# Seven more seven-product pairs in a hybrid trunk's input projection, the head groups in another order beside them, and some first accumulator writes on ScalarE

## The chip, the core and the metric

The kernel runs on one core of one Trainium2 chip. The metric is device time in microseconds (us) for one launch. TensorE (PE) multiplies, VectorE (DVE) and ScalarE (ACT) work on PE's results and on operands, GpSimd (POOL) prepares weights, SyncE (SP) issues most of the DMA transfers, ACT issues the rest from its own instruction stream. Every engine works through its instructions in order, and the orders are fixed when the kernel is built; a semaphore wait at one instruction holds everything behind it on that engine.

## What is computed

One layer of a trunk on x (1024 x 2048): a norm, one wide projection, three groups of heads, an output projection with residual, a final norm.

```python
h = rmsnorm(x, norm_gain)
proj = jnp.einsum('bsd,de->bse', h, w_in)              # 59 column tiles of 128
aq, af, ai, ag, bq, bk, bv, bg, cq, ck, cv, cg = split_columns(proj)
ya = hgrn2_group(aq, af, ai, lb, hgrn_gain) * jax.nn.silu(ag)      # A: 6 heads, recurrence
yb = band_attention_group(bq, bk, bv, rel_bias) * jax.nn.silu(bg)  # B: 5 heads, softmax
yc = retention_group(cq, ck, cv, cos, sin) * jax.nn.silu(cg)       # C: 5 heads, retention
y = jnp.concatenate([ya, yb, yc], axis=-1)
x = x + jnp.einsum('bse,ed->bsd', y, w_out)
return rmsnorm(x, final_gain)
```

An A head needs four column tiles (f, q, v, gate), a B head four (q, k, v, gate), a C head three (q and k together, v, gate).

## The kernel before

**Products.** Every large product is computed in three passes, high by high, low by high, high by low, with the operands split into `_hi` and `_lo`. A matmul instruction multiplies a 128x128 weight block by 512 columns. The tokens are two halves of 512 columns, the contraction is 16 row blocks of 128. A plain tile (128 output columns, all tokens) therefore takes 16 x 2 x 3 = 96 matmuls. A *pair* of tiles can be computed by a seven-product scheme (7 products of half the contraction, on half the tokens): 7 x 8 x 3 = 168 matmuls in place of 192. It needs sums and differences of weight blocks and of h blocks as operands, and adds the products up in accumulators in SBUF (`acc_in`).

**Stage 1** (`in_product`, L800): 15 pairs, so 105 steps of one product each, two *granules* of weights (four 128x128 blocks) per step. Product j is done for all 15 pairs in turn, since all share the operand set `in_hi[j%2]`, `in_lo[j%2]`, whose h combinations are built in SBUF for one j and overwritten for j+2. For weights with two terms (products 0 to 4 of the seven) POOL adds the terms (L753), ACT makes w_hi (L1203), DVE makes w_lo (L1697); for one-term weights POOL makes w_lo (L760). DVE accumulates (`in_accumulate`, L1747 to L1761). SP stores finished accumulators to `z_scratch`.

**Rows of h.** The plain tiles need the 16 h rows (`mv_hi`, `mv_lo`). In the last steps of stage 1 SP loads each row of x into an accumulator that its store has left (`load_x`, L572), ACT makes the high part (`h_high`, L1243), DVE the low part (`h_low`, L1766).

**Plain tiles beside the heads** (`project`, L821): the other 29 tiles, each cut into 8 *slots* of 12 matmuls. After a slot PE does whatever head stage a table has put there (`put`, L1046): A head u from slot 20u-4 on (`A_FROM`, `A_EACH`), B heads each 12 slots from slot 121, C heads at 183, 192, 201, 210 and the last at 223 to 231. An A head has one diagonal product (`a_diag`), seven levels (`a_level`), transposes, state, output and two half sums of squares (`a_ss`); between the levels DVE makes the next operand pair and drains the last result (`lv_next`, `lv_drain`). A C head has key transposes (`c_ktr`), scores, value transposes, state, output, and two half sums of squares (`c_ss`, L851 and L852). Its key is rotated first: ACT makes `partner`, DVE `rotate` (L2095 to L2099), and these stand behind the previous head's norm and gating (L1930, L1936) and an eviction (L1648). Head inputs come back from `z_scratch` by DMAs that ACT issues (`load_z`, L1262); tiles of stage 1 are scaled by rstd before they are stored, plain ones after they land (`landed`, L1655).

**Then** the output projection, in seven-product pairs as well (L1092), and the final norm.

## Time and profile before

| | us |
|---|---|
| median of 3 runs | 1776.33 (1775.26 to 1777.37) |
| the profiled execution | 1775.74 |
| its span in the trace | 1773.9 |
| PE busy | 1743.0 (98%) |
| DVE, POOL, ACT busy | 1107.9, 763.1, 626.4 |
| stage 1: PE from 8.5 to about | 603 |
| plain tiles beside the heads | about 603 to 1440 |

The profile is a page for one execution: busy time of each engine, the span in forty slices with the clock that PE was granted, the DMA queues, the chain of waits that ended last, and groups of instructions by code line. The trace behind it answers for single instructions: start, duration, and, in brackets, how long the engine was idle before and what released it. A duration printed for a matmul is longer than the distance to the next one, since they are pipelined; the distance between starts is what counts.

### The profile page before, as it was taken

The page shows a single profiled execution, that of the slowest core. Times are in us where ns is not written, and L with a number is a line of the kernel's source. Part 1 is how long each engine was busy: PE and PEld are TensorE (multiplying, and loading weights), DVE is VectorE, ACT ScalarE, POOL GpSimd, SP SyncE. Part 2 cuts the span into 40 slices and gives each one's busy share as a digit, 9 for nine tenths or more (in the row PEclk, how much of TensorE's full clock was granted, in tenths as well). Part 3 has the DMA queues.
Part 4 walks back from the last instruction along what each step waited for, and adds up shares of the span by engine and source line. Part 5 has one row for each costly group of instructions (what it writes and reads, how often), then busy time and mean ns, then how long its engine had stood idle before and what let it go on. Part 6 is the DMA issues. An engine that isn't in the chain of part 4 may idle for free.

```text
span 1773.9 us, 27559 instructions
## 1 busy us (share of the span) xinstructions
PE 1743.0 (98%) x10704; PEld 1444.8 (81%) x10704; DVE 1107.9 (62%) x1641; ACT 626.4 (35%) x923; POOL 763.1 (43%) x545
## 2 busy tenths in 40 slices
PE   7999999999999999999999999999999999999996
PEld 6888888888888788887887888888888877888885
DVE  6857665554668766565555356555655448778886
ACT  4423344332435132231331233333544233333442
POOL 4544444444455544334344433333334430355452
PEclk9999999999999999999999999999999999999998
DMA  7767777685988523323323332233433369778876
GB/s 252 231 226 255 241 236 256 226 261 179 301 268 271 168 71 126 101 74 109 113 72 102 127 109 85 96 96 112 133 117 102 93 207 344 256 247 264 282 248 230
DMA packets 160710, 323.08 MB, mean 182 GB/s; under 512 B 18362, under 2 KB 19135, under 8 KB 160580
## 3 DMA queue, kind: packets, MB, share of 16 engines
q1 hardware_dynamic: 146314, 276.26, 47.7%
q10 hardware_dynamic: 14266, 45.05, 7.2%
q8 instruction: 86, 1.41, 0.3%
q14 instruction: 44, 0.36, 0.1%
HBM read 275.08 MB, written 46.15 MB: 181 GB/s over the span
## 4 chain that ended last, share of the span: by engine, by line
PE 95%; DVE 2%; ACT 1%; DMA 1%; issue 0%; POOL 0%; SPq 0%; DVEq 0%; ACTq 0%; POOLq 0%
PE prj L821 36%; PE prj L800 32%; PE prj L1092 15%; PE mix L960 2%; PE mix L943 2%; PE mix L840 1%; PE mix L885 1%; PE mix L953 1%; PE mix L913 1%; PE mix L916 1%; PE mix L902 1%; PE mix L1013 1%; PE mix L991 1%; PE mix L1016 0%; PE mix L1002 0%; DVE arena L2245 0%
## 5 line engine op out<-in xcount | busy, mean ns | idle before, releaser
L767 POOL TENSOR_SCALAR w_hi<-w_sum 128x512 fp32r<-128x512 f32 x119 | 189.5, 1592 | 502.5 <-DMA w_sum<-in_w 490.6
L800 PE MATMUL prj<-in_hi,w_hi 128*128 128x512 f32 x840 | 329.7, 392 | 9.5 <-DVE w_lo L1697 8.5
L800 PE MATMUL prj<-in_lo,w_hi 128*128 128x512 f32 x840 | 328.4, 391 | 0.0
L800 PE MATMUL prj<-in_hi,w_lo 128*128 128x512 f32 x840 | 328.3, 391 | 0.0
L821 PE MATMUL prj<-mv_hi,w_hi 128*128 128x512 f32 x928 | 300.7, 405 | 1.8 <-DVE mv_lo L1766 1.8
L753 POOL TENSOR_TENSOR w_sum<-in_raw,in_raw 128x512 f32<-128x512 f32 x150 | 202.4, 1350 | 211.0 <-PE prj L800 201.1
L821 PE MATMUL prj<-mv_lo,w_hi 128*128 128x512 f32 x928 | 287.4, 391 | 0.0
L821 PE MATMUL prj<-mv_hi,w_lo 128*128 128x512 f32 x928 | 286.2, 390 | 0.0
L821 PEld LDWEIGHTS prj<-mv_lo,w_hi 128*128 128x128 f32 x928 | 174.2, 188 | 38.1
L821 PEld LDWEIGHTS prj<-mv_hi,w_lo 128*128 128x128 f32 x928 | 174.2, 188 | 38.0
L800 PEld LDWEIGHTS prj<-in_hi,w_hi 128*128 128x128 f32 x840 | 158.5, 189 | 44.0 <-issue 8.9
L821 PEld LDWEIGHTS prj<-mv_hi,w_hi 128*128 128x128 f32 x928 | 163.2, 188 | 29.4 <-DVE mv_lo L1766 2.2
L800 PEld LDWEIGHTS prj<-in_lo,w_hi 128*128 128x128 f32 x840 | 158.7, 189 | 33.5 <-issue 0.5
L800 PEld LDWEIGHTS prj<-in_hi,w_lo 128*128 128x128 f32 x840 | 158.7, 189 | 33.1
L1697 DVE TENSOR_TENSOR w_lo<-w_sum,w_hi 128x512 fp32r<-128x512 f32 x150 | 115.8, 775 | 111.5 <-ACT w_hi L1203 107.9
L776 POOL TENSOR_TENSOR raws<-raws 128x512 f32<-128x512 f32 x80 | 111.8, 1399 | 164.5 <-DMA raws<-in_wo 164.5
L769 POOL TENSOR_TENSOR w_lo<-w_sum,w_hi 128x512 fp32r<-128x512 f32 x124 | 171.2, 1381 | 22.8 <-ACT w_hi L1526 12.9
L1092 PE MATMUL prj<-mv_hi,w_hi 128*128 128x512 f32 x448 | 175.1, 391 | 3.8 <-POOL w_lo L769 1.2
L1092 PE MATMUL prj<-mv_lo,w_hi 128*128 128x512 f32 x448 | 174.4, 389 | 0.0
L1092 PE MATMUL prj<-mv_hi,w_lo 128*128 128x512 f32 x448 | 174.3, 389 | 0.0
L1203 ACT ACTIVATE w_hi<-w_sum 128x512 fp32r<-128x512 f32 x150 | 93.8, 628 | 175.3 <-POOL w_sum L753 175.2
L760 POOL TENSOR_TENSOR w_lo<-in_raw,w_hi 128x512 fp32r<-128x512 f32 x60 | 81.4, 1357 | 82.5 <-ACT w_hi L1203 82.4
(175 smaller groups left out, 2371.8 us busy)
## 6 DMA issues: line engine op xcount, KB each, us to landing
in_raw<-in_wi SPq DMA_DIRECT2D x360, 256.0 KB, 3.2
raws<-in_wo SPq DMA_DIRECT2D x184, 256.0 KB, 3.9
...
```

The costliest lines, as they stand in the source:

```text
L753: nc.gpsimd.tensor_tensor(w_sum[wslot(n)][:], in_raw_buf(a), in_raw_buf(b), ALU.add if sign > 0 else ALU.subtract).then_inc(in_wsum, 1)
L760: nc.gpsimd.tensor_tensor(w_lo[wslot(n)][:], in_raw_buf(m), w_hi[wslot(n)][:].bitcast(F32), ALU.subtract).then_inc(w_split, 1)
L767: nc.gpsimd.tensor_scalar(w_hi[q][:], w_sum[q][:], 1.0, None, ALU.mult).then_inc(w_hi_done, 1)
L769: nc.gpsimd.tensor_tensor(w_lo[q][:], w_sum[q][:], w_hi[q][:].bitcast(F32), ALU.subtract).then_inc(w_split, 1)
L776: nc.gpsimd.tensor_tensor(raw_buf(a), raw_buf(a), raw_buf(b), ALU.add if sign > 0 else ALU.subtract).then_inc(wsum_done, 1)
L800: last = nc.tensor.matmul(out, wt[wslot(n)][:, i % GRAN, :], mv[j % 2][:, i, :], start=(i == 0 and wt is w_hi and mv is in_hi), stop=(i == ...
L821: last = nc.tensor.matmul(prj[pair][:, half(side)], wt[wslot(q)][:, kk, :], mv[:, k, half(side)], start=(k == 0 and wt is w_hi and mv is m ...
L943: last = nc.tensor.matmul(mix[0][:, out_at + lo:out_at + hi], arena_r[:, wt, p * P:p * P + P], arena_r[:, mv, keys], start=(wt == BQH and ...
L960: last = nc.tensor.matmul(mixb(1)[:, 5, :], blocks(V)[:, p + 1 - nk + j, :], blocks(BT[p % 2])[:, j, :], start=(j == 0), stop=(j == nk - 1))
L1092: last = nc.tensor.matmul(bank(s), wt[wslot(W0 + n)][:, i % GRAN, :], slot(mv, j, i), start=(i == 0 and wt is w_hi and mv is mv_hi), stop= ...
L1203: nc.scalar.activation(w_hi[wslot(n)][:], src, ACT.Copy).then_inc(in_w_hi, 1)
L1697: tt(w_lo[wslot(n)][:], src, w_hi[wslot(n)][:].bitcast(F32), ALU.subtract).then_inc(w_split, 1)
```

## The change

Seven further pairs (`MID_PAIRS`) are computed by the seven-product scheme, after stage 1, and only 15 plain tiles are left. The operand sets for it are those of stage 1: they are stored to a DRAM scratch (`comb_scratch`, 7 x 8 x 2 blocks of 256 KB) while stage 1 uses them, and loaded back into `mv_hi`/`mv_lo` for the middle part. The middle part has 49 steps, 98 slots; with 15 x 8 = 120 plain slots the slot table has 218 entries in place of 232. Head stages now stand in the middle part's slots too, in a new order: B heads at slots 2 to 61, C heads 0 to 2 at 64, 72, 80, then the A heads at 89, 108, 125, 142, 159, 176, C head 3 at 201, and the last C head at 209 to 217. The columns of w_in are reordered to suit, and the counts of semaphores are rewritten. In the middle part POOL makes both the sum and w_lo; ACT makes w_hi and, for products 0 and 1, also writes the accumulators first (`in_first`); DVE does the other accumulations. The x rows and h rows are made at slots 88 to 103 (`H_DUE`), in the order of quarters 1, 2, 0, 3.

```diff
-A_FROM, A_EACH, B_FROM, B_EACH = -4, 20, 121, 12
-A_LATE = 2
-LEVEL_AT = [8, 9, 11, 12, 13, 15, 16]
-C_AT = [183, 192, 201, 210]
+MID_PAIRS = 7
+STD0 = IN_TILES + 2 * MID_PAIRS
+SLOTS = MID_SLOTS + 2 * NG * STD
+A_AT = [89, 108, 125, 142, 159, 176]
+LEVEL_AT = [8, 9, 10, 11, 12, 14, 15]
+LEVEL_AT_SLOW = [8, 9, 11, 12, 14, 15, 17]
+B_FROM, B_EACH = 2, 12
+C_AT = [64, 72, 80, 201]
+FIRST_ORDER = [1, 2, 0, 3]
+        H_DUE = [88, 89, 90, 91, 91, 93, 95, 97, 100, 100, 101, 101, 101, 102, 103, 103]
...
+            def store_set(j, i):
+                sp.wait_ge(in_comb_lo, HK * j + (i + 1 if j > 0 else HK))
+                for n, mv in enumerate((in_hi, in_lo)):
+                    sp.dma_start(comb_dram[j, i, n], mv[j % 2][:, i, :].bitcast(F32)).then_inc(comb_out[j % 2], 16)
...
+            load_x(HK)
+            store_mid_two(ALL_STEPS - 4)
+            load_x(HK + 1)
+            load_std_w(ALL_GRANULES)
+            store_mid_two(ALL_STEPS - 3)
+            load_x(HK + 2)
...
+            for n in range(IN_ONE, ALL_GRANULES):
+                if IN_GRANULES <= n + 1 < ALL_GRANULES and in_two(n + 1):
+                    in_weight_sum(n + 1)
+                src = w_sum[wslot(n)][:] if in_two(n) else in_raw_buf(in_raw_of[n][0])
                 pool.wait_ge(in_w_hi, n + 1)
...
-                if g < IN_TILES + 2:
-                    pe.wait_ge(in_acc_done, IN_STEPS - 1 + g - IN_TILES)
+                if g < STD0 + 2:
+                    pe.wait_ge(in_acc_done, ALL_STEPS - 2 + 2 * (g - STD0))
...
-            for slot_at, part in ((223, c_ktr), (224, c_scores), (225, c_vtr), (227, c_state), (229, c_out)):
+            for slot_at, part in ((-9, c_ktr), (-8, c_scores), (-7, c_vtr), (-5, c_state), (-3, c_out)):
+                put(SLOTS + slot_at, part(last_c))
+            for st in range(IN_STEPS, ALL_STEPS):
+                pe.wait_ge(in_acc_done, st - 3)
+                for q in range(2):
+                    mid_product(2 * st + q, range(GRAN * q, GRAN * q + GRAN))
+                    stages[2 * (st - IN_STEPS) + q]()
...
+                until(b)
+                a_z_first(u)
+                until(b + 1)
+                a_z_second(u)
+                if u == 0:
+                    load_z(a_tile(u) + 1, T1, z1_in)
+                    load_z(a_tile(u) + 2, VT, z2_in)
+                sigmoid_exp(m, Q)
+                until(b + 2)
```

On ACT, `until(slot)` puts in front of a head's next step the middle part's own work that is due by then: first writes, w_hi up to slot + 3, and h_high rows.

ACT before, where stage 1 ends and A head 0 begins (`z_clamped` to `silu_log` are the waits of that head's exponentials and logarithms, `in_raw_*` are weights of stage 1; the loads of this head's tiles stand 13 rows further up):

```order
L1243 ACTIVATE mv_hi<-acc_in,gain_sb 128x1024 [waits z_odd1]
L1137 ACTIVATE arena<-arena 128x1024 [waits z_clamped]
L1140 ACTIVATE arena<-arena 128x1024 [waits y_stored,z_exp]
L1203 ACTIVATE w_hi<-in_raw_67 128x512 [waits w_used,raw_in2]
L1203 ACTIVATE w_hi<-in_raw_68 128x512 [waits w_used,raw_in3]
L1140 ACTIVATE arena<-arena,lb_now 128x1024 [waits z_under,lb_copied]
L1137 ACTIVATE arena<-arena 128x1024 [waits z_log]
L1203 ACTIVATE w_hi<-in_raw_69 128x512 [waits w_used,raw_in4]
L1203 ACTIVATE w_hi<-in_raw_70 128x512 [waits w_used,raw_in5]
L1243 ACTIVATE mv_hi<-acc_in,gain_sb 128x1024 [waits z_odd2]
L1137 ACTIVATE arena<-arena 128x1024 [waits silu_clamped]
L1140 ACTIVATE arena<-arena 128x1024 [waits silu_exp]
```

ACT after, at the same head's beginning, which is now the end of the middle part (slots 88 to 91; `in_raw_66`, `67`, `68` are the weights of granules 303, 304, 305, that is slots 93, 94, 95):

```order
L1297 ACTIVATE arena<-arena 128x1024 [waits z_clamped]
L1300 ACTIVATE arena<-arena 128x1024 [waits z_exp]
L1363 ACTIVATE w_hi<-in_raw_66 128x512 [waits w_used,raw_in1]
L1402 ACTIVATE mv_hi<-acc_in,gain_sb 128x1024 [waits z_even2]
L1300 ACTIVATE arena<-arena,lb_now 128x1024 [waits z_under,lb_copied]
L1297 ACTIVATE arena<-arena 128x1024 [waits z_log]
L1424 DMA arena<-z_scratch 128x1024 [waits z_mid0] x2
L1297 ACTIVATE arena<-arena 128x1024 [waits silu_clamped]
L1363 ACTIVATE w_hi<-in_raw_67 128x512 [waits w_used,raw_in2]
L1402 ACTIVATE mv_hi<-acc_in,gain_sb 128x1024 [waits z_even3]
L1402 ACTIVATE mv_hi<-acc_in,gain_sb 128x1024 [waits z_mid0]
L1300 ACTIVATE arena<-arena 128x1024 [waits silu_exp]
```

The load of the head's q tile moved to right in front of the instruction that needs it, and the next w_hi (`in_raw_67`) stands behind that instruction; two h rows (`z_even3`, `z_mid0`) stand in front of the w_hi after that, which comes four instructions below the last row shown.

SP before, in the last steps of stage 1:

```order
L549 DMA in_raw_69<-in_wi 128x512 [waits w_split]
L549 DMA in_raw_70<-in_wi 128x512 [waits w_split]
L577 DMA z_scratch<-acc_in 128x512 [waits in_scaled] x2
L572 DMA acc_in<-in_xT 128x1024 [waits z_odd3]
L577 DMA z_scratch<-acc_in 128x512 [waits in_scaled] x4
L572 DMA acc_in<-in_xT 128x1024 [waits z_odd4]
```

SP after, in the last steps of the middle part (`in_acc_done` counts the steps accumulated; the four stores shown are those of steps 149, 150, 151 and, last, 152, in this order):

```order
L677 DMA z_scratch<-acc_in 128x512 [waits in_acc_done] x2
L667 DMA acc_in<-in_xT 128x1024 [waits z_even3,w_used]
L667 DMA acc_in<-in_xT 128x1024 [waits z_mid0]
L677 DMA z_scratch<-acc_in 128x512 [waits in_acc_done] x2
L667 DMA acc_in<-in_xT 128x1024 [waits z_mid1]
L709 DMA w_sum_54<-in_w 128x512 [waits w_used]
L677 DMA z_scratch<-acc_in 128x512 [waits in_acc_done] x2
L667 DMA acc_in<-in_xT 128x1024 [waits z_mid2]
L709 DMA w_sum_55<-in_w 128x512 [waits w_used]
L677 DMA z_scratch<-acc_in 128x512 [waits in_acc_done] x2
```

Both times the loads of x rows stand between stores; after, they stand behind stores of steps that are still being computed, with the first plain weights between them.

PE after, between the last half sum of squares of C head 3 (L1006, L1007) and the key transposes of the last C head (L995). Before, these transposes (L840, with the same waits) stood 36 such plain rows, six slots, behind L851 and L852; now six:

```order
L1006 MATMUL mix<-part_hi,ones 128x512 [waits parts_split]
L1007 MATMUL mix<-part_lo,ones 128x512
L976 MATMUL prj<-mv_hi,w_hi 128x512 x2
L976 MATMUL prj<-mv_lo,w_hi 128x512 x2
L976 MATMUL prj<-mv_hi,w_lo 128x512 x2
L976 MATMUL prj<-mv_hi,w_hi 128x512 x2
L976 MATMUL prj<-mv_lo,w_hi 128x512 x2
L976 MATMUL prj<-mv_hi,w_lo 128x512 x2
L995 MATMUL mix<-ident,arena 128x128 [waits mix1_drained,c_rot,const_in]
```

Five slots went out from between the two; ACT's and DVE's work between them (norm, gating, eviction, partner, rotation) is unchanged.

## Rows read from the trace of the kernel before

**Rows 1.** The page: PE's busy line; the chain that ended last.

```profile
PE 1743.0 (98%) x10704; PEld 1444.8 (81%) x10704; DVE 1107.9 (62%) x1641; ACT 626.4 (35%) x923; POOL 763.1 (43%) x545
...
PE 95%; DVE 2%; ACT 1%; DMA 1%; issue 0%; POOL 0%; SPq 0%; DVEq 0%; ACTq 0%; POOLq 0%
```

**Rows 2.** Waits of PE: line, releaser, us in total, times, longest.

```profile
PE prj L821 <- DVE mv_lo L1766: 1.8, 1, 1.8
```

**Rows 3.** Timeline, PE: start, us, line, operation, how many; plain tiles, then output projection.

```profile
807.17 0.76 PE L862 MATMUL mix<-arena 128*32 128x32 f32 x64
...
810.79 0.76 PE L885 MATMUL mix<-arena 128*32 128x32 f32 x64
...
1600.88 0.39 PE L1092 MATMUL prj<-mv_hi,w_lo 128*128 128x512 f32 x1
...
1602.01 0.39 PE L1092 MATMUL prj<-mv_lo,w_hi 128*128 128x512 f32 x1
```

**Rows 4.** Timeline, ACT, end of stage 1: h_high, an exponential, w_hi.

```profile
550.04 1.14 ACT L1243 ACTIVATE mv_hi<-acc_in,gain_sb 128x1024 fp32r<-128x1024 f32 x1
551.08 1.04 ACT L1137 ACTIVATE arena<-arena 128x1024 f32<-128x1024 f32 x1
...
553.12 0.62 ACT L1203 ACTIVATE w_hi<-in_raw 128x512 fp32r<-128x512 f32 x1
```

**Rows 5.** Timeline, DVE, end of stage 1: h_low, two accumulations.

```profile
562.91 1.28 DVE L1766 SCALAR_TENSOR_TENSOR mv_lo<-acc_in,gain_sb,mv_hi 128x1024 fp32r<-128x1024 f32 x1
...
566.64 1.28 DVE L1750 TENSOR_TENSOR acc_in<-acc_in,prj 128x512 f32<-128x512 f32 x2
```

**Rows 6.** Source L572 (x rows, 512 KB), from issue to landing.

```profile
DMA to landing us min/median/max: 3.4/5.3/8.3
```

**Rows 7.** Source L1262 (head tiles, 512 KB), from issue to landing.

```profile
DMA to landing us min/median/max: 3.1/3.9/7.9
```

**Rows 8.** Groups by line and form, DVE: count, busy us, mean ns: drains of levels.

```profile
L1857 DVE COPY_PREDICATED arena<-level,mix 128x1024 f32<-128x1024 int8 x30 | 39.6, 1319 | 0.0
```

**Rows 9.** Timeline, all engines, from C head 3's sum to the last ktr.

```profile
1397.81 0.39 PE L851 MATMUL mix<-part_hi,ones 128*128 128x512 f32 x1
...
1400.70 1.23 DVE L1930 SCALAR_TENSOR_TENSOR arena<-mix,arena 128x1024 f32<-128x1024 f32 x1 [4.06 <-ACT arena L1137]
...
1403.11 1.22 DVE L1648 TENSOR_TENSOR arena<-prj,rstd 128x1024 f32<-128x1024 f32 x1
...
1408.70 1.23 DVE L2095 TENSOR_TENSOR arena<-arena 128x1024 f32<-128x1024 f32 x1 [4.18 <-ACT arena L1478]
...
1409.84 2.32 DVE L2096 TENSOR_TENSOR arena<-arena 128x1024 f32<-128x1024 f32 x1
...
1412.19 1.22 DVE L2099 TENSOR_TENSOR arena<-arena 128x1024 f32<-128x1024 f32 x1
...
1414.59 1.04 PE L840 MATMUL mix<-ident,arena 128*128 128x128 f32 x8
```

**Rows 10.** Timeline, PE at its start: every 0.43, from 17.73 faster.

```profile
16.88 0.63 PE L800 MATMUL prj<-in_hi,w_lo 128*128 128x512 f32 x1
...
17.73 0.53 PE L800 MATMUL prj<-in_lo,w_hi 128*128 128x512 f32 x1
```

**Rows 11.** Windows: us, busy PE, PEld, DVE, ACT, POOL; clock, DMA share, GB/s.

```profile
100.00:200.00 100.00, 100.00 (x443) 82.81 (x442) 60.87 (x90) 32.22 (x53) 49.23 (x38) 1.00 0.72 234
...
1500.00:1505.00 5.00, 5.00 (x24) 4.13 (x23) 3.72 (x7) 1.75 (x3) 0.00 (x0) 1.00 1.06 388
1012.00:1251.00 239.00, 238.60 (x1311) 200.61 (x1309) 134.59 (x245) 80.95 (x153) 84.81 (x58) 1.00 0.31 101
...
1765.00:1770.00 5.00, 0.00 (x0) 0.00 (x0) 2.78 (x5) 0.00 (x0) 2.23 (x2) 0.50 1.02 381
```

**Rows 12.** The page, groups of POOL: weight sum and w_lo.

```profile
L753 POOL TENSOR_TENSOR w_sum<-in_raw,in_raw 128x512 f32<-128x512 f32 x150 | 202.4, 1350 | 211.0 <-PE prj L800 201.1
...
L769 POOL TENSOR_TENSOR w_lo<-w_sum,w_hi 128x512 fp32r<-128x512 f32 x124 | 171.2, 1381 | 22.8 <-ACT w_hi L1526 12.9
```

More of the change, by code:

```diff
@@ L206, in arr @@
             return arena[:, n, :]
-        ones_f32 = stage[:, 0:P]
+        ones_f32 = rstd[:, 0:P]
         def blocks(n):
@@ L653, in _ @@
+            store_mid_two(ALL_STEPS - 1)
+            for k in range(HK + 4, KB):
+                load_x(k)
+            for n in range(ALL_GRANULES + NG, W0):
                 load_std_w(n)
-                g, q = divmod(n - IN_GRANULES, NG)
-                t = IN_TILES + g - 2
-                if IN_TILES <= t < DIRECT and q == (0 if t == DIRECT - 1 else 1):
+                g, q = divmod(n - ALL_GRANULES, NG)
+                t = STD0 + g - 2
+                if STD0 <= t < DIRECT and q == (0 if t == DIRECT - 1 else 1):
@@ L1041, in _ @@
                     ones_product(0)
-            stages = [nothing] * (2 * NG * STD)
+            stages = [nothing] * SLOTS
             def put(slot, *parts):
@@ new lines, in a_unit @@
+                until(b + 9)
+                if u > 0:
+                    store_y(u - 1, a_pos(u - 1))
+                until(b + 10)
+                until(b + 11)
+                sigmoid_exp(m + 1)
+                sigmoid_ln(m + 1)
+                until(b + 12)
+                sigmoid_inv(m + 1)
+                for slot in range(b + 13, b + kdtr_at - 1):
+                    until(slot)
+                if u < A_HEADS - 1:
+                    act.wait_ge(silu_done, m + 2)
+                    load_z(a_tile(u + 1) + 1, T1, z1_in)
@@ L1487, in c_unit @@
             def c_unit(i):
[L1488 to L1491 removed]
+                b, m, late, end = C_AT[i], c_silu(i), i == C_HEADS - 2, i == EARLY - 1
+                until(b)
+                if i == 0:
+                    store_y(B0 + B_HEADS - 1, B_HEADS - 1)
+                elif late:
+                    store_y(A_HEADS - 1, a_pos(A_HEADS - 1))
+                else:
+                    store_y(C0 + i - 1, c_pos(i - 1))
@@ L1513, in c_unit @@
-                norm_second(A_HEADS + i + 1)
-                norm_ln(0, M0_C + C_M0 * i + 3, 16 * (C0 + i) + 16)
-                norm_exp(0, M0_C + C_M0 * i + 3)
-                evict_until(b + 6)
+                    if end:
+                        load_z(a_tile(0), B, z0_in)
+                    else:
+                        act.wait_ge(filled[1], c_m1(i) + 2)
+                        act.wait_ge(c_qd, i + 1)
+                        load_z(c_tile(i + 1), CQK, z0_in)
+                        until(b + 2)
+                        partner(i + 1)
@@ new lines, in c_unit @@
+                until(b + 2)
+                act.wait_ge(drained[0], c_m0(i) + 2)
+                if not end:
+                    act.dma_start(dec, dec_d[i + 1]).then_inc(cdec_in, 16)
+                until(b + 3)
+                if late:
+                    sigmoid(m)
+                elif not end:
+                    load_z(c_tile(i + 1) + 1, VT, z2_in)
+                until(b + 4)
+                norm_first(1, c_m1(i) + 3, m + 1, c_norm(i))
+                until(b + 5)
+                if i < EARLY - 1:
+                    scaled_k(i + 1)
+                    act.wait_ge(silu_done, m + 1)
+                    load_z(c_tile(i + 1) + 2, T1, z1_in)
```

833 lines of the change are left out of this document (479 added, 354 removed).

## The prediction

> **What bounds the kernel now.** First the page. PE is busy 98% of the span, and the chain that ended last is PE for 95% of it [rows 1]. So removed matmuls count in full, and so does every new microsecond in which PE waits. Then the waits of PE: between 20 us and the output projection it waits once, 1.8 us, for a low h row at the point where stage 1 hands over to the plain tiles [rows 2]. So that handover and the end of the head stages have no slack to speak of before, and these are the two places to read closely. Last the timeline, for the distance between matmuls: from 1600.88 to 1602.01 are five, 0.226 us each; from the diagonal's stage at 807.17 to the next stage at 810.79 lie one slot of 12 matmuls (2.72) and the 64 small matmuls of a stage (0.90) [rows 3]. The span is 1773.9 and the execution 1775.74, 1.8 more; the median of the runs is 1776.3. I sum against 1775.7.
>
> **What goes away.** Seven pairs at 168 in place of 192 matmuls save 168 matmuls, 14 slots: 168 x 0.2267 = **-38.1**. Head stages are the same in number and form. The old 1.8 us wait [rows 2] belongs to a handover that no longer exists: **-1.8**.
>
> **The new handover, slots 88 to 106.** It now holds four things that all go through ACT and DVE in a fixed order: norm of C head 2, last steps of the middle part, all 16 h rows, and A head 0's first tiles. I walk through it with the order of the instructions in the section on the change and durations from before: a wide exponential or logarithm on ACT 1.04, w_hi 0.62, h_high 1.14, all about 0.1 less from start to start [rows 4]; h_low 1.28, a step's two accumulations 1.28 [rows 5]; a POOL w_lo 1.38 [rows 12]; x rows land 5.3 after issue (3.4 to 8.3) [rows 6], head tiles 3.9 (3.1 to 7.9) [rows 7]. Time zero is PE's end of slot 88; PE's own plan is slot 94 at 13.6, slot 98 at 24.5, level 6 of A head 0 at 54.9 (18 slots, plus the stages between).
> - C head 2's norm leaves DVE at 2.2, an accumulation and the clamps of A's f tile at 5.8. ACT does exponential and logarithm, one w_hi and one h_high, then the second pair: done at 13.2. Only now is the q tile's load issued (before it stood 13 rows ahead). It lands at 17.2; DVE scales and clamps it, 19.0.
> - ACT has been held at the sigmoid of this tile until then, and the w_hi of slot 94 stands behind it: 20.7, w_lo 22.0. PE wanted it at 13.6: 8.4 late.
> - DVE accumulates step 149 only behind the head's log f, at 22.9. SP's next x rows stand behind the store of that step: issued at 23.8, landed 29.1. ACT makes two h_high (31.3), three sigmoid parts (34.5), and then the w_hi of slot 95: w_lo at 36.4. PE has reached slot 95 at 24.7, so 11.7 more.
> - Slots 95 to 97 run to 44.5. The first plain tile waits for the accumulation of step 151, which stands behind silu, step 150 and an h row: 48.8 where the plan was 24.5, **24 late in all**. The row x10 is loaded behind the store of step 151: lands at 55, h_low at 57.3, needed three slots into the tile: 27 late.
> - From there DVE has to do up to level 6: nine h_low (11.5), two steps (2.6), some fourteen half-width operand products of 0.64 (9) [rows 5], five masked drains of 1.32 (6.6) [rows 8], the gate and v tiles. That is 33, against PE's remaining 22 or so: up to **37 late** by level 6.
>
> Part of it will overlap better than I walk it: with landings at their minimum the first plain tile comes some 6 earlier, and if no x row is late, what is left is DVE's load alone, at least 15. With landings at the maximum it is over 40. I take **+34**, near the median row, bounds 15 and 42.
>
> **The last C head.** Before, C head 3's sum of squares is on PE at 1397.81; ACT's norm frees DVE at 1400.70, the eviction runs from 1403.11, ACT's partner frees the rotation at 1408.70, and it ends at 1412.19 + 1.22 = 1413.4; the transposes start at 1414.59 [rows 9]. That is 16.8 from sum to transposes, over six slots (16.3 plus a few tenths), and nothing is lost. After there is one slot between them, 2.72 and the second sum's two matmuls, 3.2. The chain is no shorter, and it starts from the same PE instruction. PE stands still for the slack-free chain less this: 15.6 - 3.2 = **+12.4**; 11.3 if the 2.32 at 1409.84 is 1.2 next time [rows 9]. Nothing else on PE can fill it, as PE goes in order. If A5's last slots have left ACT late it is a few more.
>
> **The clock after a wait.** In the first ten microseconds of work after the idle start matmuls came every 0.43, up to 17.73 [rows 10]: 21 of them from 8.48, each 0.2 dearer, 4.2 in all. Near the end, with PE idle, the granted clock of a stretch was 0.50 [rows 11], which is 1.2 in place of 2.4 GHz. Waits of 8 to 12 us may bring that on once or twice. Nothing (the 1.8 us wait did not show it) to 8; I take one time, **+4**.
>
> **What else moves.** (a) Stage 1 stores its combinations: 112 blocks of 256 KB, 29.4 MB, and the middle part reads them back. Stage 1 moves 234 GB/s at a share of 0.72 now [rows 11]; in 8 of every 15 steps another 512 KB in some 5.4 us a step is 97 GB/s, so near 330, below the 388 seen at share 1.06. Covered, but nearly without slack at bursts: 0 to 15, I take 0. (b) B heads beside the middle part: DVE is busy 134.6 of 239 there, ACT 81, POOL 85 [rows 11]. DVE gets 2 to 4 accumulations a step instead of nothing, ACT a w_hi and some first writes, POOL 1.35 + 1.38 per slot of about 4.0 [rows 12]. All below full; 0 to 3, I take 1. (c) C heads 0 to 2 at 8 in place of 9 slots: their chain from sum to the next key is not overlapped better than before: 0 to 5, I take 2. (d) First writes on ACT in place of DVE and A heads at 17 slots in place of 20: the A heads' DVE work no longer has slack at every level; 0 to 3, taken 0. (e) Reordered columns and the new counts move no work. Together **+3**.
>
> A rule to weigh here: one of the DVE rows above took 1.23 and the next of the same form 2.32, beside a POOL instruction [rows 9]. The Trainium skill (SBUF — State Buffer, "SBUF: two separate sides") says that a DVE instruction with two SBUF inputs and a GpSimd instruction exclude each other for the whole length of the first. The two rows agree with that, as far as two rows can.
>
> **Sum.** 1775.7 - 38.1 - 1.8 + 34 + 12.4 + 4 + 3 = 1789.2; the walk of the handover leaves more room down than up, so I forecast **1787**.
>
> **Rivals.**
> - *The handover costs half* (ends on the other side). If loads land near their minimum, 3.4 and 3.1 [rows 6, 7], and DVE fills its waits, A head 0 is late by 15 to 22 only, as DVE's load alone asks. 1775.7 - 39.9 + 18 + 11.3 + 1 = **1766**. It decides itself at a handover wait below 24: above, the kernel is not faster. For it: PE hides 6 or 7 us wherever a slot boundary absorbs a wait twice counted. Against: two x-row loads stand one behind the other, each behind an accumulation. Chance 0.24.
> - *Between the two*: a handover of 24 to 30 cancels the saving, **1776**. Chance 0.10.
> - *The full saving*: both waits do not appear, because some instruction is earlier than I read it: 1775.7 - 38.1 = **1738**. The order against it is plain at the last C head. Chance 0.04.
> - *The operand sets collide with the weights.* If the stores of stage 1 push weight loads over the limit in 8 of 15 steps for seven products, or a set for the middle part (4 MB) is late, PE waits some 0.3 to 0.5 per step, 20 to 40 us: **1815**. For it: 388 GB/s is all that was seen [rows 11], at peak. Against: three raw blocks stand ahead per granule. Chance 0.10.
> - *DVE and POOL in each other's way.* With POOL busy in 2.73 of 4.0 us of a slot, five wide DVE instructions of a C head at +1.09 each [rows 9] make 5.5 for each of three C heads, and about as much for B's operand lows: +15 on top of the forecast, **1800**. It decides if DVE reaches 90% there. By the skill's rule named above it is this case. Chance 0.10.
>
> **Chances.** The forecast's own case (both waits near what I walked, 1775 to 1800) has 0.42. A measurement of this kernel tells 0.2%, 3.5 us, from no change. Faster: 0.24 + 0.04 = 0.28. Same: 0.10, the case between. Slower: 0.42 + 0.10 + 0.10 = 0.62. The range takes in the half-price handover and the DVE case and part of the operand-set case: 1760 to 1806; outside it lie the full saving and most of the collision, some 0.13, and a little for the ends.
>
> **What would show it.** (1) Matmul instructions fall by 168. (2) The waits of PE show a row for w_lo from POOL of 8 and more us near slot 94, one more at slot 95, and one for in-step accumulations or h_low before the first plain tile; their sum with A head 0's levels is 34. (3) One wait of 11 to 13 us for the rotation at c_ktr (L995), after C head 3. (4) A clock below 1.00 in a window right behind one of them. (5) Stage 1 ends at the same time as before, within 2 us. It is wrong if (2) is under 24 in sum, since the rest of the sum then gives a faster kernel; if stage 1 is longer, the transfers did it; if B's stretch has waits on DVE, the DVE case.

## The result

| | before | after |
|---|---|---|
| median of 4 runs, us | 1776.7 (1775.3 to 1777.4) | 1803.5 (1803.1 to 1804.0) |
| the profiled execution, its span | 1775.7, 1773.9 | 1803.3, 1801.5 |

The ratio after to before is 1.0152, 95% interval 1.0135 to 1.0170: 26.8 us slower. The forecast was 1787, slower by 11, with a range of 1760 to 1806. The sign and the range hold; the forecast size is less than half of what was measured.

First the page of the changed kernel (its busy line and its chain, against [rows 1]), then the waits of PE: line, releaser, us in total, times, longest.

```profile
PE 1723.3 (96%) x10536; PEld 1422.7 (79%) x10536; DVE 1172.9 (65%) x1721; ACT 680.5 (38%) x1037; POOL 846.1 (47%) x601
...
PE 52%; DVE 6%; issue 2%; ACT 2%; DMA 2%; SPq 0%; ACTq 0%; POOL 0%; DVEq 0%
```

```profile
PE mix L995 <- DVE arena L2324: 11.3, 1, 11.3
PE prj L939 <- DVE w_lo L1916: 8.9, 1, 8.9
PE mix L1040 <- DVE arena L2052: 8.8, 4, 7.7
PE prj L954 <- DVE acc_in L1971: 7.9, 2, 4.6
PE prj L976 <- DVE mv_lo L1987: 7.4, 4, 4.5
PE prj L954 <- POOL w_lo L899: 7.3, 1, 7.3
PE mix L995 <- DVE arena L2172: 1.9, 2, 0.9
PE mix L1098 <- ACT arena L1332: 1.6, 3, 0.7
```

PE has 168 matmuls fewer (10536 for 10704) and is busy 20 us less, not 38. Of the rows shown, the only one that was there before too is the start (L939, 8.9). All the others stand where before there was one wait of 1.8 [rows 2].

Where the time went can be read to a few tenths from the starts of the matmuls in PE's timeline: every twelfth large matmul starts a slot, so each slot has a length. Stage 1 ends at 587.5 (before 587.3, and not at the 603 of the table ahead of the prediction), and from the first matmul of the output projection to the end of the span it takes 328.6 (before 328.5). All of it lies between. That stretch was 858.1 long; less the 38.1 and the 1.8 it should be 818.2, and it is 885.5: **67.3 us lost**. The loss of each stretch, against the same stages' slots of before (an A head's stages cost 14.5 beyond its slots, a B head takes 50.75, a C head's nine slots 34.0), is:

| stretch | slots | over PE's own work | the prediction said |
|---|---|---|---|
| B heads | 2 to 61 | 3.9 | 1 |
| C head 0 comes in | 62 to 64 | 5.2 | nothing of its own |
| C heads 0 to 2, rest | 65 to 88 | 3.0 | 2 |
| handover to A head 0 | 89 to 107 | 38.7 | 34, and 4 for the clock |
| A heads 1 to 5 | 108 to 192 | 2.6 | 0 |
| last C head | 208 to 217 | 13.9 | 12.4 |

The two places that the prediction named, the handover and the last C head, hold 52.6 of the 67.3. PE's timeline at these places, with the idle time before a start and its releaser in brackets:

```profile
859.67 0.47 PE L954 MATMUL prj<-mv_hi,w_hi 128*128 128x512 f32 x1 [3.34 <-DVE acc_in L1971]
...
979.24 0.77 PE L954 MATMUL prj<-mv_hi,w_hi 128*128 128x512 f32 x1 [4.57 <-DVE acc_in L1971]
991.75 0.80 PE L954 MATMUL prj<-mv_hi,w_hi 128*128 128x512 f32 x1 [7.33 <-POOL w_lo L899]
...
1015.58 1.08 PE L1040 MATMUL mix<-arena 128*32 128x32 f32 x64 [7.67 <-DVE arena L2052]
...
1439.68 1.94 PE L995 MATMUL mix<-ident,arena 128*128 128x128 f32 x8 [11.26 <-DVE arena L2324]
```

Slot 88 ends at 960.9, so 979.24 is slot 94, 991.75 slot 95. ACT's timeline shows what holds the w_hi of these slots: a sigmoid's exponential (L1297) that waits for DVE's clamp, one w_hi, then two h rows that wait 7.3 for their landing, a logarithm and two exponentials (the forget gate's is one of them), and only then the next w_hi (three in one row). At slot 94 two things came last together: POOL's w_lo behind that w_hi ended at 979.14, DVE's accumulation, behind the head's log f, at 979.20.

```profile
975.52 1.06 ACT L1297 ACTIVATE arena<-arena 128x1024 f32<-128x1024 f32 x1 [2.23 <-DVE arena L1877]
976.48 0.61 ACT L1363 ACTIVATE w_hi<-in_raw 128x512 fp32r<-128x512 f32 x1
984.41 2.43 ACT L1402 ACTIVATE mv_hi<-acc_in,gain_sb 128x1024 fp32r<-128x1024 f32 x2 [7.32 <-DMA acc_in<-in_xT]
...
989.74 1.65 ACT L1363 ACTIVATE w_hi<-in_raw 128x512 fp32r<-128x512 f32 x3
```

And the clock, in windows of 5 us (busy time of PE, PEld, DVE, ACT, POOL, then granted clock, DMA share, GB/s), at the handover and at the last C head:

```profile
970.00:975.00 5.00, 4.67 (x21) 3.54 (x19) 1.43 (x2) 3.14 (x3) 0.88 (x1) 1.00 0.70 248
975.00:980.00 5.00, 0.76 (x2) 0.70 (x3) 4.90 (x6) 1.57 (x2) 1.97 (x1) 0.71 0.00 0
980.00:985.00 5.00, 4.42 (x12) 3.10 (x10) 1.59 (x2) 0.58 (x1) 0.00 (x0) 0.61 0.96 311
...
990.00:995.00 5.00, 3.25 (x8) 2.58 (x9) 5.00 (x5) 1.39 (x3) 4.57 (x3) 0.50 0.04 15
```

```profile
1440.00:1445.00 5.00, 5.00 (x17) 4.24 (x16) 2.77 (x4) 0.67 (x1) 0.00 (x0) 0.53 0.77 203
```

In 980 to 985 PE did 12 matmuls in 4.4 us, at full clock it does 12 in 2.7. Of the 38.7 that the handover lost, 27.3 are waits and the rest, some 11, are nearly all matmuls at the lower of the two clock levels (0.43 apart in place of 0.23).

### The profile page after: what moved, and what is told of

Same layout as the page of the kernel before. It is cut to its first block, busy times and chain, and to the rows that moved or that the text cites. A ratio compares the mean times of both kernels' runs of the same rounds, so it can differ in the third digit from the quotient of the medians.

```text
span 1801.5 us, 28210 instructions
## 1 busy us (share of the span) xinstructions
PE 1723.3 (96%) x10536; PEld 1422.7 (79%) x10536; DVE 1172.9 (65%) x1721; ACT 680.5 (38%) x1037; POOL 846.1 (47%) x601
## 4 chain that ended last, share of the span: by engine, by line
PE 52%; DVE 6%; issue 2%; ACT 2%; DMA 2%; SPq 0%; ACTq 0%; POOL 0%; DVEq 0%
PE prj L976 17%; PE prj L1252 15%; PE prj L954 9%; PE mix L1115 2%; PE mix L1098 1%; PE mix L995 1%; DMA acc_in<-in_xT 1%; PE mix L1040 1%; PE mix L1108 1%; PE mix L1068 1%; PE mix L1071 1%; PE mix L1057 1%; PE mix L1168 1%; DVE arena_r L2191 1%; PE mix L1146 0%
## 5 line engine op out<-in xcount | busy, mean ns | idle before, releaser
L888 POOL TENSOR_TENSOR w_sum<-in_raw,in_raw 128x512 f32<-128x512 f32 x220 | 307.3, 1397 | 294.7 <-PE prj L939 148.6
L939 PE MATMUL prj<-in_hi,w_hi 128*128 128x512 f32 x840 | 329.6, 392 | 9.9 <-DVE w_lo L1916 8.9
L939 PE MATMUL prj<-in_lo,w_hi 128*128 128x512 f32 x840 | 328.3, 391 | 0.0
L939 PE MATMUL prj<-in_hi,w_lo 128*128 128x512 f32 x840 | 328.3, 391 | 0.0
L906 POOL TENSOR_SCALAR w_hi<-w_sum 128x512 fp32r<-128x512 f32 x63 | 105.3, 1671 | 275.6 <-DMA w_sum<-in_w 246.1
L899 POOL TENSOR_TENSOR w_lo<-in_raw,w_hi 128x512 fp32r<-128x512 f32 x88 | 121.2, 1382 | 163.3 <-ACT w_hi L1363 163.3
L1363 ACT ACTIVATE w_hi<-w_sum 128x512 fp32r<-128x512 f32 x220 | 135.6, 626 | 164.6 <-POOL w_sum L888 160.4
L939 PEld LDWEIGHTS prj<-in_hi,w_hi 128*128 128x128 f32 x840 | 158.6, 189 | 44.3 <-issue 9.4
L939 PEld LDWEIGHTS prj<-in_lo,w_hi 128*128 128x128 f32 x840 | 158.7, 189 | 33.2 <-issue 0.5
L939 PEld LDWEIGHTS prj<-in_hi,w_lo 128*128 128x128 f32 x840 | 158.6, 189 | 33.2
L1252 PE MATMUL prj<-mv_hi,w_hi 128*128 128x512 f32 x448 | 175.1, 391 | 3.9 <-POOL w_lo L908 1.3
L954 PE MATMUL prj<-mv_hi,w_hi 128*128 128x512 f32 x392 | 162.3, 414 | 15.2 <-DVE acc_in L1971 7.9
L1252 PE MATMUL prj<-mv_hi,w_lo 128*128 128x512 f32 x448 | 174.3, 389 | 0.0
L1252 PE MATMUL prj<-mv_lo,w_hi 128*128 128x512 f32 x448 | 174.3, 389 | 0.0
L1916 DVE TENSOR_TENSOR w_lo<-w_sum,w_hi 128x512 fp32r<-128x512 f32 x150 | 111.9, 758 | 89.2 <-ACT w_hi L1363 86.2
L976 PE MATMUL prj<-mv_hi,w_hi 128*128 128x512 f32 x480 | 159.1, 413 | 7.7 <-DVE mv_lo L1987 7.4
L954 PE MATMUL prj<-mv_hi,w_lo 128*128 128x512 f32 x392 | 155.7, 397 | 0.0
L954 PE MATMUL prj<-mv_lo,w_hi 128*128 128x512 f32 x392 | 155.3, 396 | 0.0
L976 PE MATMUL prj<-mv_lo,w_hi 128*128 128x512 f32 x480 | 151.3, 397 | 0.0
L976 PE MATMUL prj<-mv_hi,w_lo 128*128 128x512 f32 x480 | 150.0, 394 | 0.0
L1971 DVE TENSOR_TENSOR acc_in<-acc_in,prj 128x512 f32<-128x512 f32 x176 | 114.1, 680 | 53.8 <-PE prj L939 53.7
```

The costliest lines, as they stand in the source:

```text
L888: nc.gpsimd.tensor_tensor(w_sum[wslot(n)][:], in_raw_buf(a), in_raw_buf(b), ALU.add if sign > 0 else ALU.subtract).then_inc(in_wsum, 1)
L899: nc.gpsimd.tensor_tensor(w_lo[wslot(n)][:], src, w_hi[wslot(n)][:].bitcast(F32), ALU.subtract).then_inc(w_split, 1)
L906: nc.gpsimd.tensor_scalar(w_hi[q][:], w_sum[q][:], 1.0, None, ALU.mult).then_inc(w_hi_done, 1)
L939: last = nc.tensor.matmul(out, wt[wslot(n)][:, i % GRAN, :], mv[j % 2][:, i, :], start=(i == 0 and wt is w_hi and mv is in_hi), stop=(i == ...
L954: last = nc.tensor.matmul(out, wt[wslot(n)][:, i % GRAN, :], slot(mv, j, i), start=(i == 0 and wt is w_hi and mv is mv_hi), stop=(i == HK ...
L976: last = nc.tensor.matmul(prj[pair][:, half(side)], wt[wslot(q)][:, kk, :], mv[:, k, half(side)], start=(at == 0 and wt is w_hi and mv is ...
```

## Experiments

Two theories on the handover. *Chain*: the instructions are lined up badly on ACT, and with another order the time comes back. *Load*: DVE has that much to do before level 6 of head A0, and the order matters little. All kernels below are the changed kernel with the edit shown; the gains are against its 1803.5. The kernel before, measured anew beside each group, had medians from 1774.8 to 1777.7, so a gain read across groups is good to 1 or 2 us; by the ratios to the kernel before, x1_last gains 10, x3_act 5 and x4_hand 15.

### The last C head: rotation ahead of the norm

```diff
                 until(b + 3)
                 if late:
+                    partner(i + 1)
                     sigmoid(m)
...
                     c_part_low(i, 0)
                     c_part_low(i, 1)
+                    rotate(i + 1)
...
-                    partner(i + 1)
                     scaled_k(i + 1)
```

The eviction of its first tile moves up too, behind C head 3's states.

> The changed kernel with one thing different: the last C head's q and k tile is evicted, its partner made and the rotation done before C head 3's norm and gating, not behind them. Theory (the order put the rotation behind the norm, with one slot of cover): the wait of 11.3 at the key transposes shrinks to the 0.9 that the other C heads show there for the drained bank, and with it goes the slow clock behind it; 13.9 lost in the last ten slots becomes about 1. Time 1803.5 - 12.5 = 1791. Rival (VectorE or ScalarE is short of time there anyway, so the wait only moves to C head 3's sums or to the states): less than 5 comes back, 1799 or more.

Measured: 1791.3. The last ten slots take 38.6 in place of 50.6, which is 1.9 over PE's own work; slot 207, in front of them, takes 1.1 more. The transposes wait for the bank, as those of C heads 1 and 2 do, and the matmuls behind it keep their distance:

```profile
1429.96 1.06 PE L995 MATMUL mix<-ident,arena 128*128 128x128 f32 x8 [1.73 <-DVE arena L2172]
```

So 11 of the 13.9 at this place were the rotation behind the norm, with the slow matmuls that followed the wait, and not scarce time on ACT or DVE.

### C head 0: due work between the steps of its set-up

```diff
+            until(62)
             partner(0)
+            until(63)
             act.wait_ge(filled[1], c_m1(0))
             zero_halves()
+            until(64)
             scaled_k(0)
...
+            until(62)
             dve.wait_ge(ctab_in, 32)
             rotate(0)
```

> The changed kernel with the middle part's own due work (w_hi on ScalarE, accumulations on VectorE) put in between the steps with which C head 0 is set up, where none was. Theory A: the 3.34 wait at slot 64, which the profile gives to an accumulation, and the 1.7 of slow clock behind it come from this, 1803.5 - 5 = 1798.5. Theory B (head set-up itself is late): the wait moves to C head 0's key transposes, 1803 to 1802.

Measured: 1802.9, which can't be told from 1803.5. The wait at slot 64 is gone, and PE waits at C head 0's key transposes, one slot on:

```profile
861.88 1.94 PE L995 MATMUL mix<-ident,arena 128*128 128x128 f32 x16 [3.00 <-issue]
```

Slots 62 to 64 take 13.2 for 15.2, the slots behind them 0.8 more. In the changed kernel the accumulation that the wait is named after ended at 859.64 and POOL's w_lo, behind a w_hi that stood behind the set-up, at 859.57: both due works were late. With them in front, the set-up is late. ACT's partner begins 3.4 later, and DVE's three rotation instructions take 1.23, 2.32 and 2.17 where each had taken 1.22. The likely reason, not tested by itself, is that partner, zeroing, rotation and decay of a head's keys start only when the last B visit is done, two slots before the transposes are due. Before there were two slots as well, but no w_hi and no accumulations in them.

### ACT's order alone

Three w_hi stand ahead of the sigmoid, and two h rows one slot later.

```diff
-        H_DUE = [88, 89, 90, 91, 91, 93, 95, 97, 100, 100, 101, 101, 101, 102, 103, 103]
+        H_DUE = [88, 89, 90, 92, 92, 93, 95, 97, 100, 100, 101, 101, 101, 102, 103, 103]
...
+                    for _ in range(3):
+                        in_w_high(due["hi"])
+                        due["hi"] += 1
                 sigmoid_exp(m, Q)
                 until(b + 2)
```

> The changed kernel with ScalarE's order alone altered at the handover to the A heads: the w_hi of slots 94 to 96 stand before the sigmoid that waits for a landing, and two h rows stand one slot later. Theory chain (the 38.7 us of that handover are waits lined up on ScalarE): the waits of 4.6 and 7.3 at slots 94 and 95 go and, with the slow clock behind them, 12 to 17 come back, 1787 to 1791. Theory accumulations (VectorE's accumulations and the x rows behind them set the time at which the first plain tile can start): the wait moves to slot 98, 0 to 5 come back, 1798 to 1803.

Measured: 1797.5, 6.0 back, between the two. The 12 us of waits at slots 94 and 95 are gone, and new ones stand at slot 96 (2.67, in front of the diagonal's stage) and at slots 97 and 98:

```profile
993.89 0.79 PE L954 MATMUL prj<-mv_hi,w_hi 128*128 128x512 f32 x1 [4.89 <-POOL w_lo L899]
1000.92 0.73 PE L976 MATMUL prj<-mv_hi,w_hi 128*128 128x512 f32 x2 [1.54 <-DVE acc_in L1974]
1011.86 1.08 PE L1040 MATMUL mix<-arena 128*32 128x32 f32 x64 [7.93 <-DVE arena L2055]
```

The w_hi of slots 94 and 95 was what PE met first, not what held it. The level stage in slot 98 still waits 7.9.

### ACT's order, early accumulations, early q tile

```diff
                 until(b)
+                if u == 0:
+                    load_z(a_tile(u) + 1, T1, z1_in)
+                    load_z(a_tile(u) + 2, VT, z2_in)
                 a_z_first(u)
...
+                if u == 0:
+                    steps_to(A_AT[0] + 1)
                 silu_landed(a_tile(u) + 1, a_silu(u), Q)
...
                 a_logf(u)
+                if u == 0:
+                    steps_to(b + 5)
                 until(b + 2)
```

`steps_to(slot)` does on DVE the accumulations that are due, without h rows; a third one (b + 7) follows the q tile's silu.

> As the run before it, and two more things: VectorE accumulates steps 149 to 152 as soon as it gets there, in front of head 0's next steps, so that stores and x rows go out earlier, and the q tile of A head 0 is loaded before its exponentials and not behind. Theory chain: all of the handover that is not VectorE's own load goes; VectorE was busy 70.8 of the 95 us from slot 88 to level 6 where PE needs 61, so about 10 of the 38.7 stay, 1803.5 - 28 = 1775. Theory load (VectorE and the transfers need the time anyway): at most 12 come back, 1791 or more.

Measured: 1787.5, 16.0 back, again between. The stretch from slot 89 to 106 takes 79.9 for 94.5. Its window in the changed kernel, and then in this one:

```profile
961.00:1055.00 94.00, 66.75 (x639) 51.07 (x639) 68.55 (x79) 33.19 (x35) 33.49 (x21) 0.82 0.54 184
```

```profile
960.00:1040.00 80.00, 62.71 (x650) 48.76 (x649) 71.47 (x80) 32.92 (x34) 34.67 (x22) 0.89 0.62 215
```

DVE was busy for 68.6 of 94 and is busy for 71.5 of 80. So part of the wait was order, and the rest looks like load. The next two ask that directly.

### More work for DVE, fewer landings

```diff
                 dve.wait_ge(h_hi, s + 1)
+                if s >= 4:
+                    nc.vector.tensor_reduce(extra[:, s, :], x_row(k), AX_X, ALU.max)
```

> The reordered handover of x4_hand (1787.5), and VectorE does one useless maximum over the x row (128x1024, some 1.2 us) in front of each of the last twelve low h rows: 14 us more of work for VectorE in that stretch and nothing else. Load theory (what is left of the handover, 24 us beyond PE's own work, is VectorE's work): nearly all of it shows, 1787.5 + 12 = 1799. Chain theory (what is left are waits for landings of x rows, with VectorE idle in them): it fits into the waits, 1788 to 1792.

Measured: 1794.6, 7.1 more than x4_hand, in the middle of the two expectations; the stretch to slot 107 takes 90.6 for 84.4. The added work was as large as meant (12 instructions, mean near 1.21, 14.5 in all):

```profile
L1993 DVE TENSOR_REDUCE extra<-acc_in x12: 1198/1209/1219, 988.8 to 1038.6; 128x1 f32<-128x1024 f32 x12
```

All twelve lie in the stretch, yet DVE's busy time in it rose from 71.5 to 78.9 only, by 7.4. Everything else that it does there became shorter by 7 in sum. The low h rows in that stretch, in x4_hand and then here (count, busy us, mean ns):

```profile
L1991 DVE SCALAR_TENSOR_TENSOR mv_lo<-acc_in,gain_sb,mv_hi 128x1024 fp32r<-128x1024 f32 x16 | 24.7, 1579 | 0.8 <-ACT mv_hi L1402 0.8
```

```profile
L1994 DVE SCALAR_TENSOR_TENSOR mv_lo<-acc_in,gain_sb,mv_hi 128x1024 fp32r<-128x1024 f32 x16 | 21.4, 1345 | 0.0
```

One such row took 1.28 alone [rows 5]. So the time rose by what DVE's busy time rose by (7.1 and 7.4), which is what a bound on DVE would do. That part of its busy time is the lengthening of instructions beside GpSimd's is a third theory, *contention*, for x11_whi_act below.

The counterpart takes landings away:

```diff
-                sp.dma_start(x_row(k), xT[k]).then_inc(x_row_sem(k), 16)
+                if not HK <= k < HK + GRAN:
+                    sp.dma_start(x_row(k), xT[k]).then_inc(x_row_sem(k), 16)
```

> The reordered handover of x4_hand, and x rows 8 to 11 are not loaded: ScalarE and VectorE make h rows 8 to 11 from whatever lies in those accumulators, once it has been stored. This leaves out those four transfers and their landing time of 5 us each, and nothing of the work. Chain theory: 5 to 12 come back, 1776 to 1782. Load theory: 0 to 3, 1785 to 1787.5.

Measured: 1788.7, no less than the 1787.5 with the transfers. This kernel leaves out the loading of four x rows, so it multiplies with what lay there. Four landings of 5 us each are worth nothing once the order is right. Chain falls as far as these four rows go, load stands.

### Both repairs together, and then less work before each slot

> The earlier rotation of x1_last and the reordered handover of x4_hand together. They lie 400 us apart on PE, so they should add up: 1803.5 - 12.2 - 16.0 = 1775.3, no different from the kernel before. If the handover's gain was only room that the end then ate, less: 1780.

Measured: 1776.3, ratio to the kernel before 1.0007 (0.9997 to 1.0016). The two repairs add up, and together they take back the 27 us by which the change was slower. They don't empty the two places: the handover still loses 23.3 and the last C head 3.0. With some 14 lost elsewhere that is all that the 168 matmuls save.

```diff
-                if st >= ALL_STEPS - 4:
-                    load_x(GRAN + st - ALL_STEPS + 4)
+                if st == ALL_STEPS - 4:
+                    load_x(GRAN)
+                    load_x(GRAN + 1)
+                if st == ALL_STEPS - 3:
+                    load_x(GRAN + 2)
+                    load_x(GRAN + 3)
+                if st == ALL_STEPS - 1:
+                    load_x(HK)
...
-            load_x(HK)
...
+        H_DUE = [86, 87, 88, 88, 92, 93, 95, 97, 100, 100, 101, 101, 101, 102, 103, 103]
```

> As x7_both, and x rows 4 to 7, whose places are free from slot 84 on, are loaded in two steps in place of four, and their h rows are made one to three slots earlier, beside the end of C head 2. Load theory: four h rows (5.1 of VectorE, 4.6 of ScalarE) leave the tight stretch, 1775.3 - 4 = 1771. Chain theory: the rows that set the time are 8 to 11, unchanged, 1775. A loss is possible: C head 2's norm behind an h row that waits for its landing, 1778.

Measured: 1773.0, ratio 0.9991 (0.9981 to 1.0000), 3.3 less than x7_both; the two intervals overlap slightly, but slots 89 to 107 take 80.7 for 83.6. The gain is what load asked, though the time lies midway between the two numbers expected. Rows 8 to 11, which chain named, kept their places in the order, but with less work in front of them the loads of rows 10 and 11 went out 2.5 to 3 us earlier after slot 88 (20.7 and 25.3 for 23.8 and 27.8). So this run alone does not part the two theories; x6_nox does.

```diff
-                    if n == 2:
+                    if n == (5 if u == 0 else 2):
                         silu_landed(a_tile(u) + 3, a_silu(u) + 1)
-                    if n == 3:
+                    if n == (4 if u == 0 else 3):
                         landed(a_tile(u) + 2, VT, z2_in, a_pos(u) + 1).then_inc(v_ready, 1)
-                    if n == 4:
+                    if n == (6 if u == 0 else 4):
                         silu_finish(a_silu(u) + 1, GATE, 1.0)
```

ACT's sigmoid of that gate tile moves behind the last h rows too.

> As x8_xearly, and head A0's gate and v tiles are scaled two to three levels later, its gate's sigmoid on ScalarE behind the last h rows. The work is the same; 5.6 us of VectorE's come after the last quarter of h rows (slots 103, 104), where PE waited 4.5 and 2.4. Load theory, in the form that only the work due before each slot counts: 4 to 6 come back, 1773 - 5 = 1768. If the total up to level 6 counts, nothing: 1773.

Measured: 1769.0, ratio 0.9965 (0.9952 to 0.9977). This is faster than the kernel before, by 6.4 us, and 34.5 us faster than the change as it was made. What is left of its waits:

```profile
PE mix L1045 <- DVE arena L2063: 6.7, 3, 5.7
PE prj L981 <- DVE mv_lo L1998: 5.0, 3, 3.0
PE mix L1000 <- DVE arena L2192: 3.6, 3, 1.7
PE prj L959 <- DVE acc_in L1982: 3.3, 1, 3.3
```

Its handover takes 78.1 for the 99.0 of the changed kernel and the 60.3 of PE's own work.

> As x9_gate with the change of x2_c0 on top, whose gain of about 0.6 could not be told from nothing: 1767.5 to 1768 if it adds up; the same as x9_gate within 1 otherwise. Shows also whether the slow stretch at slots 63 and 64 (5 us over PE's own work) is C head 0's set-up itself.

Measured: 1769.0, the same as x9_gate. Slot 63 falls from 6.2 to 2.7 and slot 64 rises from 4.5 to 8.9 (1.5 of it slow matmuls), so the edit of x2_c0 again only moves the wait from a slot's first matmul to the head's transposes.

### Less of GpSimd beside DVE

```diff
+                while due["plain"] < PLAIN_ACT and MID_SLOTS - 1 + 2 * due["plain"] <= slot:
+                    plain_high(due["plain"])
+                    due["plain"] += 1
                 while due["row"] < KB and H_DUE[due["row"]] <= slot:
                     h_high(due["row"])
```

`plain_high` makes one plain granule's w_hi on ACT, four of them in all, and POOL leaves these four out.

> As x9_gate, and the w_hi of the first four plain granules (slots 98 to 105) are made by ScalarE (0.6 us each) in place of GpSimd (1.5 to 2.5 each). In x5_twice 14.5 us of added one-input work raised VectorE's busy time by only 7.4, because its two-input instructions became shorter: low h rows 24.7 to 21.4 in sum, others 3.8. Contention theory (part of VectorE's load at the handover is waiting beside GpSimd's instructions): with some 6 us of GpSimd's work taken from that stretch VectorE's instructions shorten, 2 to 4 us come back, 1769 - 3 = 1766. If contention costs nothing on the path: 1769. If h rows get late behind w_hi on ScalarE: 1771.

Measured: 1768.2, ratio to the kernel before 0.9946 (0.9933 to 0.9960), against 0.9965 of x9_gate; the two intervals overlap, so the runs alone don't settle a gain. In the profiled executions slots 89 to 107 take 73.4 for 78.1, but this one was the fastest of its five (1764.7). The same 68 us window in x9_gate and then here:

```profile
960.00:1028.00 68.00, 55.83 (x612) 43.12 (x611) 64.79 (x71) 26.75 (x27) 35.33 (x21) 0.90 0.65 232
```

```profile
960.00:1028.00 68.00, 58.05 (x646) 44.67 (x644) 62.21 (x77) 28.66 (x31) 28.24 (x18) 0.97 0.68 237
```

POOL is busy 7.1 less, DVE 2.6 less although it does six instructions more, PE 34 matmuls more at a clock of 0.97 for 0.90. DVE's instructions did shorten: in this window the twelve operand products (128x512, L2062 and L2063, here L2072 and L2073) take 8.6 for 10.8 and the 15 low h rows 21.0 for 22.0. So contention was part of DVE's load. Of the 4.7 that the stretch gains, 2.1 are something else: slots 104 and 105 take 9.9 for 12.0 behind the same wait (2.98 and 3.00), since only in x9_gate did the clock fall there. That leaves 2.6, at slots 97 to 99, for the edit. The wait there is 3.4 for 5.7; that these w_hi are also ready sooner when ACT makes them is a rival that no run separates.

The Trainium skill (SBUF — State Buffer, "SBUF: two separate sides") has one of the two engines blocked for the whole instruction of the other. The longest low h row took 2.33 in the changed kernel and 2.42 in x5_twice, for 1.28 alone, so about 1.1 added beside GpSimd instructions of 1.3 to 2.5; the rows agree with it as a worst case. Over the 16 h rows the price was 0.1 to 0.3 each.

## Why the prediction came out short

- **What goes away** held: 168 matmuls, the old wait. With everything repaired that could be, 6 to 10 of the 39.9 reached the end (x9_gate, x11_whi_act).
- **The handover** was walked at 37 to level 6 and taken at 34, with 4 for the clock: 38. Measured 38.7. That the two agree is luck: the waits were 27.3 for 34 and the slow matmuls 11 for 4, and the two errors cancel. The q tile was issued at 9.4 after slot 88's end, not at 13.2, as a transfer's issue on ACT does not wait for the two activations in front of it (last section). That carried 4.5 us down the line: w_hi of slot 94 done at 16.2 for 20.7, x rows issued at 19.2 for 23.8, the first plain tile at 44.0 for 48.8. Level 6 was done at 94.5 for 92; 11 of it are slow matmuls, which the walk did not have. The walk named the order of waits rightly, and their sum stayed above the 24 below which it was to be wrong. It would not have shown that the repair of the order is worth only 15 of the 38.7; the sentence that DVE's load alone asks at least 15 is near what the runs leave (x4_hand 24, x9_gate 18, x11_whi_act 13).
- **The last C head** at 12.4 measured 11.3 of wait, as the walk had it for a rotation without the 2.32 (it took 1.22 this time), and 13.9 with the slow matmuls behind it. x1_last gives 12.2 back (10 by the ratios).
- **The clock, taken at +4, is one of the two steps that failed.** I gave it one occasion, since I believed only waits of 8 to 12 us could bring it on. It came after waits of 3.34, 4.57 and 4.52 too. Slow matmuls make up some 11 of the 38.7 at the handover, 1.7 of the 5.2 at slot 64, 2.6 of the 13.9 at the end, so between 15 and 16 in all. Part of its size is chance: the wait of 3.34 at slot 64 recurs in nine of the other runs, and in three of them (x6_nox, x9_gate, x11_whi_act) no slow matmul follows. It did not break the handover's sum because the waits there were shorter than walked; that slow matmuls fill time in which PE would have waited for DVE anyway is a likely reason, which no run tests.
- **"What else moves", taken at +3, is the other.** These stretches lost 14.7 (3.9 in B, 5.2 and 3.0 in C, 2.6 in A), 13.0 without the slow matmuls at slot 64. For (b) I read busy shares, all below full, and took 1. A share can't show that a head's step and the middle part's step stand in line on one engine: three waits for ACT's copy at B heads (L1098, 1.6 in sum) are such. For (c) I had the eight slots of C heads, but not the two slots in which head 0 is set up beside due w_hi; that junction alone was 5.2. For (d) I took 0 where A heads at 17 slots lose 0.3 to 0.8 each. Of these only the junction was tried in runs (x2_c0, x10_gate_c0), and neither brought it back; why the rest is lost is read from the waits.
- **Sum and forecast.** 53.4 was the total of my losses and 67.3 the real one. Term by term: handover waits 27.3 for 34, last C head 11.3 for 12.4, clock 15 to 16 for 4, what else moves 13.0 for 3. Two terms too small by 12 and 10 stand against one too large by 7 and one by 1. I then took 2 off for "more room down than up", without a row. That makes up the 16 us by which 1787 falls short of 1803.5. With waits as long as walked the time would have been some 1811, outside the range, so that it lies inside is luck in part.
- **The rivals.** The half-price handover (18 for 34) and the full saving did not occur. The operand sets did not collide: stage 1 was at 587.5 for 587.3, although its transfers rose to a share of 0.99 between 50 and 100 us (0.70 before). DVE and POOL in each other's way did not add 5.5 at each of the three C heads (5.2 and 3.0 over all three, for the reasons above) but was a part of the handover. The 2.32 that the prediction took from rows 9 does have a POOL instruction beside it in the trace, a w_lo of 2.17 from 1408.90, which the rows don't show. In the handover three h_low rows took 5.05, 1.7 each, beside POOL's w_hi and w_lo:

```profile
1035.37 5.05 DVE L1987 SCALAR_TENSOR_TENSOR mv_lo<-acc_in,gain_sb,mv_hi 128x1024 fp32r<-128x1024 f32 x3 [0.83 <-ACT mv_hi L1402]
```

Open: how the 39 us split exactly into order, DVE's work and contention, since repairing one changes the others. By the lengths of slots 89 to 107 it is 15 for order (x4_hand), 3 and 3 for work moved out from before the slots (x8_xearly, x9_gate), 3 for contention and 2 for the clock (x11_whi_act), and 13 are left.

## What to carry to other kernels

When a change takes slots away from under a table of stages, count for each chain between two stages how many slots of cover it had and has: here a chain of 15.6 us over one slot cost nearly all of its difference (11.3 of 12.4), while DVE's busy share over the whole kernel was 65%. A wait repaired where PE meets it first moves to where the load is (12 us of waits gone, 6 us gained), so add up the work that an engine must have done before each slot, and give the gain only down to that. Price every junction between groups, not only the groups: here four stretches at 3 to 5 us each made up near half of the error, and slow matmuls behind new waits the rest. When a sum of several terms comes out right, check the terms one by one: two of them may be wrong in opposite ways.

## What the runs showed of the chip

The granted clock fell within a wait of 4.57 us (0.71 in the window that holds it), and after one of 3.34 us the matmuls came every 0.43 us from 1.5 us on:

```profile
860.90 0.47 PE L954 MATMUL prj<-mv_hi,w_lo 128*128 128x512 f32 x1
861.17 0.63 PE L954 MATMUL prj<-mv_hi,w_hi 128*128 128x512 f32 x1
861.60 0.63 PE L954 MATMUL prj<-mv_lo,w_hi 128*128 128x512 f32 x1
```

Those are 1.2 in place of 2.4 GHz, and the slot they stand in took 6.1 for 4.4. The same wait in x9_gate had no such end, its twelve matmuls took 2.8 and the slot 4.5:

```profile
858.74 0.47 PE L959 MATMUL prj<-mv_hi,w_hi 128*128 128x512 f32 x1 [3.33 <-DVE acc_in L1982]
...
861.57 1.91 PE L1000 MATMUL mix<-ident,arena 128*128 128x128 f32 x16
```

After the 1.73 us wait of x1_last the transposes took 1.06 for the 1.94 of the changed kernel, at full clock. The Trainium skill (TensorE: Matmul & The Clock Gate, "Part 1: The HAM clock gate") says that the throttled state is the default and activity releases it; the rows here agree. For an estimate this means: here a new wait of three to five microseconds cost between nothing and 2.6 us more than itself, for one and the same wait from one execution to the next, and the waits above seven some 2 to 3 each, where PE was the bound behind them.

A transfer that ACT issues goes out before activations that stand in front of it have begun. In the order of the changed kernel the load of the q tile stands behind a logarithm (L1300) and an exponential (L1297); in ACT's timeline it is issued first:

```profile
970.27 0.81 ACTq L1424 DMA_DIRECT2D arena<-z_scratch  x2
971.21 1.14 ACT L1300 ACTIVATE arena<-arena,lb_now 128x1024 f32<-128x1024 f32 x1
972.25 1.04 ACT L1297 ACTIVATE arena<-arena 128x1024 f32<-128x1024 f32 x1
```

So such a place in ACT's order says which semaphores must have come, not that the work ahead of it is done.
